# DeltaNet's raw keys, queries and values turned by a DMA exchange through DRAM and VectorE block transposes in place of TensorE transposes

## The chip, the core and the metric

The kernel runs on one core of a Trainium2 chip. A core has a matrix engine (TensorE, PE in the profile), a vector engine (VectorE, DVE), an activation engine (ScalarE, ACT), a general engine (GpSimd, POOL), a queue engine that here only issues transfers (SyncE, SP) and 16 DMA engines between DRAM and the on-chip memory SBUF. TensorE writes to a second on-chip memory, PSUM, that VectorE and ScalarE read. The engines run their own instruction streams and meet at semaphores. The metric is the device time of one execution in microseconds (us).

## The reference, cut to what matters here

One decoder layer over 256 tokens of width 2048: a gated DeltaNet branch with 16 heads of 128 and a sliding-window attention branch, merged by gates, then an output projection and a squared-ReLU MLP. The part that the change touches is the way of queries, keys and values from their projection to the depthwise convolution over time:

```python
def causal_depthwise_conv(x, w):           # w has CONV_K = 4 taps per channel
    return lax.conv_general_dilated(
        x, w[:, None, :].astype(x.dtype), window_strides=(1,), padding=[(w.shape[0] - 1, 0)],
        dimension_numbers=("NWC", "WIO", "NWC"), feature_group_count=x.shape[-1])

h = rms_norm(x, norm1_g[l])
proj = h @ w_in[l]
qkv_g, z, b_logit, a_logit, q_s, k_s, v_s, gate_logits = jnp.split(proj, split_points, axis=-1)
# gdn_branch:
qkv_c = jax.nn.silu(causal_depthwise_conv(qkv, conv_w))
q, k, v = jnp.split(qkv_c, 3, axis=-1)
q = l2_normalize(heads(q))
k = l2_normalize(heads(k))
o = gated_delta_rule(q, k, heads(v), g, beta)
```

The projection leaves tokens on partitions and channels along the row; the convolution works along the tokens with one weight per channel, so its input is wanted with channels on partitions.

## The kernel before

All weights arrive as 584 chunks of 128x1024 floats (512 KB) in a ring of four buffers `raw`. ScalarE rounds a chunk to `w_hi` (L776), VectorE subtracts to get the rest `w_lo` (L1176, the function `split`), and TensorE multiplies three times, in `product`: hi by hi (L347), hi activations by `w_lo` (L348), lo activations by `w_hi` (L349). Both other engines are `AHEAD = 3` chunks ahead of the chunk whose jobs they do. An output of 512 columns takes 8 chunks; its sums stand in one of two halves of PSUM's `acc`.

The first 16 outputs are four windows `w` = 0 to 3 of four outputs each: keys, queries, values and the gate z of one group of four heads. At the end of an output ScalarE (first 128 tokens, L1036) and VectorE (the other 128, L1584) copy it scaled to `rawg[:, n]`. The work on the heads of group g runs between the matmuls of window g + 1, at places given by tables: TensorE counts a step `s` for every three matmuls of `product` (128 in a window; a chunk is four), the other two count `h`, half as fast (64 in a window). `k_step` is also called with `s - 128` and `h - 64`, so a key step at -8 stands 8 steps before the end of the window that makes the keys.

For each item (keys K, queries Q, values V) of a group the way is this. `turn_group` on TensorE transposes `rawg[:, n]` in eight 128x128 pieces into two PSUM banks `J` (L404), at `PE_FRONT`: K at -8, Q at 17, V at 54. `conv` on ScalarE makes the first tap from `J` (L832, four instructions), `tap` on VectorE adds three more taps (L1207, four instructions each), for K at h = -5, 0 and 4. ScalarE takes a tanh (L849), `silu` on VectorE multiplies (L1213), and `turn_units` on TensorE turns the result back (L411), at `PE_BACK`: K at 17, directly ahead of the turn of Q; then come norms and the delta rule's inverse. That inverse goes in five levels: TensorE multiplies (L435, at `PE_INV_V`), VectorE adds (L1220), TensorE squares (L445), VectorE writes under masks (L1226 to L1230), and the next level's L435 waits for that. The L435 of level 2 (they count from 0) is at s = 55, one step behind the turn of V. Later steps are products with the state (`PE_P1` L526, `PE_P2` L540, `PE_P3` L550), which VectorE prepares (L1348) and takes up (L1361, L1366), a final scale that waits for a GpSimd power (L1378), and the turn of the outputs with its rounded parts (L1388 on VectorE).

SyncE issues chunk c as soon as VectorE has split chunk c - 4 (L321 in `stream`).

Of the kernel before, what the change touches and what calls it, by code (L numbers as in the profile page):

```python
# [20 lines left out]
ALU = mybir.AluOpType  # L21
# [13 lines left out]
HG = 4  # L35
# [33 lines left out]

PE_FRONT = {ITEM_K: -8, ITEM_Q: 17, ITEM_V: 54}  # L70
PE_BACK = {ITEM_K: 17, ITEM_Q: 49, ITEM_V: 80}
# [37 lines left out]
def hybrid_trunk(nc, x, weights, w_ba, colp_d, rowp_d, masks_d, dist_d, fgain_d, out):  # L109
    with ExitStack() as ctx:  # L110
# [56 lines left out]
        with ExitStack() as mlp:  # L167
# [92 lines left out]
        def over(a, n, b=None):  # L260
# [16 lines left out]
        rawg_a, rawg_d, cw_ready, par_ready = sem("rawg_a"), sem("rawg_d"), sem("cw_ready"), sem("par_ready")  # L277
        front_T, conv_0, conv_tap, tanh_done, silu_done, back_T = (
            sem(n) for n in ("front_T", "conv_0", "conv_tap", "tanh_done", "silu_done", "back_T"))
        vb_done, nsq_done, nssq_done, nr_link, nr_done, norm_done = (  # L280
# [27 lines left out]
        @block.sync  # L308
        def _(sp):
            for i in range(4):  # L310
                sp.dma_start(raw[:, i], weights[i]).then_inc(raw_in[i], 16)
                for n in ((0, 1) if i == 0 else (i + 1,)):
                    cols = X_COLS[n]
                    sp.dma_start(xres[:, :, cols], x[:, :, cols]).then_inc(x_in[n], 16)

            def stream(a, b):
# [8 lines left out]
            stream(1, first_swa)  # L325
# [15 lines left out]
        def _(pe):  # L341
# [57 lines left out]

            def turn_group(src, b0, sem_, dst_cols=None):  # L400

                for m in range(HG):
                    for t in range(NT):
                        ins = tr(J[:, b0 + m // 2, (m % 2) * T + t * P:(m % 2) * T + (t + 1) * P],  # L404
                                 src[:, t, m * P:(m + 1) * P], ident)
                ins.then_inc(sem_, 1)

            def turn_units(b0, src, done):
# [5 lines left out]
            def k_step(s, g):  # L414

                if s == PE_FRONT[ITEM_K]:
                    pe.wait_ge(rawg_a, 4 * g + 1)
                    pe.wait_ge(rawg_d, 4 * g + 1)

                    pe.wait_ge(o_done, NCH * g + NCH)  # L420
                    turn_group(rawg[:, ITEM_K], BANK[ITEM_K], front_T)
                if s == PE_BACK[ITEM_K]:
                    pe.wait_ge(silu_done, 4 * g + 1)
                    turn_units(0, kU, back_T)
# [33 lines left out]
            def gdn_step(s, g):  # L458
# [6 lines left out]
                if s == PE_KK:  # L465
# [4 lines left out]
                    inner(0, False, kk_done)  # L470
                if s == PE_FRONT[ITEM_Q]:
                    pe.wait_ge(rawg_a, 4 * g + 2)
                    pe.wait_ge(rawg_d, 4 * g + 2)

                    pe.wait_ge(exp_done, g + 1)
                    turn_group(rawg[:, ITEM_Q], 2, front_T)
# [7 lines left out]
                if s == PE_FRONT[ITEM_V]:  # L484
                    pe.wait_ge(rawg_a, 4 * g + 3)
                    pe.wait_ge(rawg_d, 4 * g + 3)

                    pe.wait_ge(nsq_done, 2 * g + 2)
                    turn_group(rawg[:, ITEM_V], 2, front_T)
                if s == PE_BACK[ITEM_V]:  # L490
# [273 lines left out]
        def _(act):  # L764
# [63 lines left out]
            def conv(n, g, dst):  # L828

                act.wait_ge(front_T, 3 * g + (n + 1))  # L830
                for m in range(HG):
                    ins = A(dst[:, m], J[:, BANK[n] + m // 2, (m % 2) * T:(m % 2 + 1) * T], ACT.Copy,  # L832
                            scale=cwg[:, n, m, 3:4])
                ins.then_inc(conv_0, 1)
# [186 lines left out]
            def window(q0, jobs):  # L1021
                for n in range(4):
                    def ops(n=n):
# [11 lines left out]
                        else:  # L1035
                            A(rawg[:, n, 0], acc[:, n % 2, 0], ACT.Copy, scale=row_scale(0, 0)).then_inc(rawg_a, 1)  # L1036
                    output(q0 + n * (CPO // RING), jobs, read(q0 + (n + 1) * (CPO // RING), ops), h0=16 * n,
# [24 lines left out]
            for n in range(5):  # L1062
                def ops(n=n):
                    if n == 0:

                        act.wait_ge(front_T, 3 * NG - 2)
                        A(kdup[:, 0].rearrange("p (k d c) -> p k d c", k=4, d=2),
# [98 lines left out]
        def _(dve):  # L1166
# [32 lines left out]
            def tap(n, s, g, dst):  # L1199
# [5 lines left out]
                for m in range(HG):  # L1205
                    b, o = BANK[n] + m // 2, (m % 2) * T
                    ins = stt(out=dst[:, m, s:T], in0=J[:, b, o:o + T - s], scalar=cwg[:, n, m, 3 - s:4 - s],  # L1207
                              in1=dst[:, m, s:T], op0=ALU.mult, op1=ALU.add)
# [13 lines left out]
            def write_xu(lv, g):  # L1222
# [669 lines left out]
```

## Time and profile before

| | |
|---|---|
| median of 3 runs | 1782.39 us (1782.3 to 1782.4) |
| the profiled execution | 1781.72 us, its span 1779.8 us |
| TensorE busy | 1762.3 us (99%), granted clock 0.999 |
| VectorE busy | 1264.3 us (71%) |
| ScalarE busy | 853.1 us (48%) |
| GpSimd busy | 96.3 us (5%) |
| bytes moved by DMA | 316.49 MB, mean 178 GB/s |

Busy time is the union of an engine's instructions. Matmuls overlap, since the next one enters before the last has drained; a 512-column matmul is shown with about 0.39 us but the next begins about 0.23 us after it, so a short stop of TensorE can hide under the tail of the matmul before. The four windows of DeltaNet's projections end at about 109, 226, 344 and 461 us of the span; the work on group 3 runs on to about 575 us beside the next outputs.

### The profile page before, as it was taken

Reading aid. Unit: us, or ns where it says so; the run is one execution under the profiler, and the core shown is the slowest. Engines: PE = TensorE matmul, PEld = TensorE weight load, DVE = VectorE, ACT = ScalarE, POOL = GpSimd, SP = SyncE. Lnnn points to the kernel's source line nnn. Section 1 sums busy time; section 2 is a strip of 40 time slices with the busy share of each in tenths; the row PEclk is TensorE's granted clock in tenths of the full one; section 3 lists DMA queues with packets and bytes.
Section 4 is the critical chain, followed back from the end, with each engine's and each line's share of the span. In section 5 each row is a group of like instructions: output and inputs, shape, how many; then the busy total and the mean of one; then the engine's idle time right before and its main releaser. Section 6 shows DMA issues by size and latency. Waiting matters only on the chain.

```text
span 1779.8 us, 27113 instructions
## 1 busy us (share of the span) xinstructions
PE 1762.3 (99%) x9974; PEld 1432.9 (81%) x9974; DVE 1264.3 (71%) x1903; ACT 853.1 (48%) x1345; POOL 96.3 (5%) x81
## 2 busy tenths in 40 slices
PE   8999999999999999999999999999999999999998
PEld 6887787777777888888888888888888888888886
DVE  5578688787886677775676697888644468886444
ACT  6454454554645455554444454454443345444443
POOL 0021030030210000000000000000000000000000
PEclk9999999999999999999999999999999999999999
DMA  7544444444444545445666565555666555556554
GB/s 265 176 156 133 155 151 138 160 143 143 137 136 161 178 153 168 155 154 187 204 210 201 198 217 186 192 189 195 205 191 197 192 192 194 192 189 198 192 191 140
DMA packets 88118, 316.49 MB, mean 178 GB/s; under 512 B 9728, under 2 KB 10496, under 8 KB 87888
## 3 DMA queue, kind: packets, MB, share of 16 engines
q1 hardware_dynamic: 86608, 311.20, 52.6%
q0 software_dynamic: 832, 3.15, 0.5%
q8 instruction: 73, 1.20, 0.3%
q10 hardware_dynamic: 576, 0.71, 0.1%
q14 instruction: 29, 0.24, 0.0%
HBM read 312.92 MB, written 2.10 MB: 177 GB/s over the span
## 4 chain that ended last, share of the span: by engine, by line
PE 93%; DVE 6%; issue 1%; ACT 0%; DMA 0%; POOLq 0%; POOL 0%; ACTq 0%; DVEq 0%
PE acc L347 29%; PE acc L348 28%; PE acc L349 28%; DVE cT L1207 2%; DVE w_lo L1176 1%; PE J L526 1%; PE J L578 1%; PE J L411 1%; PE J L404 1%; PE J L435 1%; PE J L540 1%; PE J L455 0%; PE J L550 0%; PE J L597 0%; PE J L445 0%
## 5 line engine op out<-in xcount | busy, mean ns | idle before, releaser
L1176 DVE TENSOR_TENSOR w_lo<-raw,w_hi 128x1024 fp32r<-128x1024 f32 x584 | 712.5, 1227 | 352.5 <-ACT w_hi L776 349.7
L776 ACT ACTIVATE w_hi<-raw 128x1024 fp32r<-128x1024 f32 x584 | 617.0, 1062 | 648.2 <-PE acc L349 641.3
L347 PE MATMUL acc<-w_hi,hT_hi 128*128 128x512 f32 x1440 | 577.3, 401 | 2.3 <-DVE w_lo L1176 1.5
L348 PE MATMUL acc<-w_lo,hT_hi 128*128 128x512 f32 x1440 | 562.7, 391 | 0.0
L349 PE MATMUL acc<-w_hi,hT_lo 128*128 128x512 f32 x1440 | 561.9, 390 | 0.0
L347 PEld LDWEIGHTS acc<-w_hi,hT_hi 128*128 128x128 f32 x1440 | 270.7, 188 | 67.4 <-issue 7.0
L349 PEld LDWEIGHTS acc<-w_hi,hT_lo 128*128 128x128 f32 x1440 | 270.9, 188 | 57.8
L348 PEld LDWEIGHTS acc<-w_lo,hT_hi 128*128 128x128 f32 x1440 | 271.1, 188 | 52.7 <-issue 1.0
L347 PE MATMUL acc<-w_hi,act_hi 128*128 128x512 f32 x512 | 199.2, 389 | 0.0
L348 PE MATMUL acc<-w_lo,act_hi 128*128 128x512 f32 x512 | 199.2, 389 | 0.0
L349 PE MATMUL acc<-w_hi,act_lo 128*128 128x512 f32 x512 | 199.2, 389 | 0.0
L1483 DVE STREAM_TRANSPOSE nat<-rbuf 32x256 f32<-32x256 f32 x256 | 111.5, 435 | 4.1
L348 PEld LDWEIGHTS acc<-w_lo,act_hi 128*128 128x128 f32 x512 | 96.1, 188 | 20.0
L349 PEld LDWEIGHTS acc<-w_hi,act_lo 128*128 128x128 f32 x512 | 96.1, 188 | 20.0
L347 PEld LDWEIGHTS acc<-w_hi,act_hi 128*128 128x128 f32 x512 | 96.1, 188 | 19.9
L347 PE MATMUL acc<-w_hi,og_hi 128*128 128x512 f32 x256 | 100.5, 392 | 0.0
L349 PE MATMUL acc<-w_hi,og_lo 128*128 128x512 f32 x256 | 99.7, 389 | 0.0
L348 PE MATMUL acc<-w_lo,og_hi 128*128 128x512 f32 x256 | 99.7, 389 | 0.0
L347 PEld LDWEIGHTS acc<-w_hi,og_hi 128*128 128x128 f32 x256 | 48.1, 188 | 11.1 <-issue 1.3
L349 PEld LDWEIGHTS acc<-w_hi,og_lo 128*128 128x128 f32 x256 | 48.1, 188 | 10.1
L348 PEld LDWEIGHTS acc<-w_lo,og_hi 128*128 128x128 f32 x256 | 48.1, 188 | 9.7
L347 PE MATMUL acc<-w_hi,os_hi 128*128 128x512 f32 x128 | 49.8, 389 | 0.0
(234 smaller groups left out, 1341.1 us busy)
## 6 DMA issues: line engine op xcount, KB each, us to landing
raw<-weights SPq DMA_DIRECT2D x584, 512.0 KB, 3.4
xres<-x POOLq DMA_DIRECT2D x4, 512.0 KB, 4.8
xres<-x SPq DMA_DIRECT2D x3, 512.0 KB, 8.9
y<-nat SPq DMA_DIRECT2D x6, 256.0 KB, 3.7
fgain_sb<-fgain SPq DMA_DIRECT2D x1, 1024.0 KB, 5.5
masks_sb<-masks POOLq DMA_DIRECT2D x1, 704.0 KB, 8.1
xres<-x SPq DMA_DIRECT2D x2, 256.0 KB, 5.3
y<-nat ACTq DMA_DIRECT2D x2, 256.0 KB, 3.1
```

The source lines that it names most:

```text
L347: mm(o, aT_hi[:, kt, tok], w_hi[:, c % RING, w], start=first, stop=False)
L348: mm(o, aT_hi[:, kt, tok], w_lo[:, c % RING, w], start=False, stop=False)
L349: return mm(o, aT_lo[:, kt, tok], w_hi[:, c % RING, w], start=False, stop=last)
L404: ins = tr(J[:, b0 + m // 2, (m % 2) * T + t * P:(m % 2) * T + (t + 1) * P], src[:, t, m * P:(m + 1) * P], ident)
L411: ins = tr(J[:, b0 + u // HG, (u % HG) * P:(u % HG + 1) * P], src[:, u * P:(u + 1) * P], ident)
L435: ins = mm(J[to, bank, a * C:(a + 1) * C], lhs[r, 2 * a + b], rhs[r, 2 * a + b], start=True, stop=True)
L526: ins = mm(J[rows(par ^ q), 0, (2 * q + m) * P:(2 * q + m + 1) * P], head(src, c, 2 * m + par), S[:, 2 * m + par], start=True, stop=True)
L540: ins = mm(J[rows(par ^ q), bank, m * P:(m + 1) * P], solve[r, 2 * c + m, q], RH[r, m * P:(m + 1) * P] if c else vb3[r, m], start=True, st ...
L776: A(w_hi[:, slot], raw[:, slot], ACT.Copy).then_inc(hi_ready, 1)
L1176: tt(w_lo[:, slot], raw[:, slot], w_hi[:, slot].bitcast(F32), ALU.subtract).then_inc(lo_ready, 1)
L1207: ins = stt(out=dst[:, m, s:T], in0=J[:, b, o:o + T - s], scalar=cwg[:, n, m, 3 - s:4 - s], in1=dst[:, m, s:T], op0=ALU.mult, op1=ALU.add)
L1483: return V.transpose(dst[to * Q:(to + 1) * Q].rearrange("p (a t q n) -> p q t a n", a=4, t=NT, q=P // Q)[:, at], src[at * Q:(at + 1) * Q]. ...
```

## The change

TensorE's `turn_group` goes, with the table `PE_FRONT`. The copies of an output to `rawg` (K, Q, V) now write each quarter of 32 channels of the four heads side by side. SyncE writes `rawg[:, n]` to a DRAM buffer (`front_write`, one DMA of 512 KB) at chunk 17, 25 or 33 counted from the window's first, and two chunks later reads it back (`front_read`, eight DMAs of 32 partitions x 4 runs x 512 bytes) with partition quarters and channel quarters exchanged, into the last four rows of `og_hi` or `og_lo`, which no group but the last uses. VectorE then transposes all blocks of 32x32 with one instruction of 128x1024 (`take_front`), back into `rawg[:, n]`, at h = 37 (K), 46 (Q) and 61 (V) of the window that makes them. `conv` and `tap` read that in SBUF and not `J`.

```diff
-PE_FRONT = {ITEM_K: -8, ITEM_Q: 17, ITEM_V: 54}
+DVE_FRONT = {ITEM_K: 37, ITEM_Q: 46, ITEM_V: 61}
+SP_OUT, SP_BACK = (17, 25, 33), (19, 27, 35)
+        fronts = [a[:, 12:16].rearrange("p a t -> p (a t)").bitcast(F32) for a in (og_hi, og_lo)]
+        bounce = [nc.dram_tensor(f"bounce{i}", (P, NT * NB), F32, kind="Internal").ap() for i in range(2)]
...
+            def front_write(k):
+                w, n = divmod(k, 3)
+                sp.wait_ge(rawg_a, 4 * w + n + 1)
+                sp.wait_ge(rawg_d, 4 * w + n + 1)
+                if k > 1:
+                    sp.wait_ge(front_T, k - 1)
+                sp.dma_start(bounce[k % 2], rawg[:, n].rearrange("p t n -> p (t n)")).then_inc(front_out, 16)
+            def front_read(k):
+                sp.wait_ge(front_out, 16 * (k + 1))
+                if k:
+                    sp.wait_ge(front_T, k)
+                kept = bounce[k % 2].rearrange("(q j) (t p f) -> j p t q f", j=Q, t=NT, p=P // Q)
+                for p in range(P // Q):
+                    for t in range(NT):
+                        sp.dma_start(fronts[k % 3 % 2][p * Q:(p + 1) * Q].rearrange("j (t q f) -> j t q f", t=NT, q=P // Q)[:, t],
+                                     kept[:, p, t]).then_inc(front_in, 16)
...
-                if s == PE_FRONT[ITEM_K]:
-                    pe.wait_ge(rawg_a, 4 * g + 1)
-                    pe.wait_ge(rawg_d, 4 * g + 1)
-
-                    pe.wait_ge(o_done, NCH * g + NCH)
-                    turn_group(rawg[:, ITEM_K], BANK[ITEM_K], front_T)
...
-                    ins = A(dst[:, m], J[:, BANK[n] + m // 2, (m % 2) * T:(m % 2 + 1) * T], ACT.Copy,
-                            scale=cwg[:, n, m, 3:4])
+                    ins = A(dst[:, m], front(n)[:, m], ACT.Copy, scale=cwg[:, n, m, 3:4])
...
-                            A(rawg[:, n, 0], acc[:, n % 2, 0], ACT.Copy, scale=row_scale(0, 0)).then_inc(rawg_a, 1)
+                            A(by_quarter(rawg[:, n, 0]), by_head(acc[:, n % 2, 0]), ACT.Copy,
+                              scale=row_scale(0, 0)).then_inc(rawg_a, 1)
...
-                    ins = stt(out=dst[:, m, s:T], in0=J[:, b, o:o + T - s], scalar=cwg[:, n, m, 3 - s:4 - s],
+                    ins = stt(out=dst[:, m, s:T], in0=front(n)[:, m, 0:T - s], scalar=cwg[:, n, m, 3 - s:4 - s],
...
+            def take_front(n, g):
+                k = 3 * g + n
+                dve.wait_ge(front_in, 16 * 8 * (k + 1))
+                V.transpose(front(n).rearrange("p m (b j) -> p b m j", j=Q),
+                            fronts[n % 2].rearrange("p (b m i) -> p b m i", m=HG, i=Q)).then_inc(front_T, 1)
+
             def k_step(h, g):
+                for n in (ITEM_K, ITEM_Q, ITEM_V):
+                    if h == DVE_FRONT[n] - STEPS:
+                        take_front(n, g)
```

Where the three new instructions fall is seen at three places. The first is VectorE at the end of window 1, from the final scale of group 0 (L1378) to the rounded outputs (L1388); L1176 is `split`, L1207 the first tap on K of group 1. Before:

```order
L1378 SCALAR_TENSOR_TENSOR qn<-qn,rg,zs 128x128 [waits silu_done,or_done]
L1378 SCALAR_TENSOR_TENSOR qn<-qn,rg,zs 128x128 x7
L1176 TENSOR_TENSOR w_lo<-raw,w_hi 128x1024 [waits hi_ready]
L1207 SCALAR_TENSOR_TENSOR cT<-J,cwg,cT 128x255 [waits conv_0]
L1207 SCALAR_TENSOR_TENSOR cT<-J,cwg,cT 128x255 x3
L1176 TENSOR_TENSOR w_lo<-raw,w_hi 128x1024 [waits hi_ready] x2
L1388 SCALAR_TENSOR_TENSOR og_lo<-J,colp_sb,og_hi 128x256 [waits og_hi_done,o_T]
```

And the same place in the changed kernel, whose lines are numbered anew (L1412 is the scale, L1201 `split`, L1231 the tap, L1264 `take_front`):

```order
L1412 SCALAR_TENSOR_TENSOR qn<-qn,rg,zs 128x128 x7
L1201 TENSOR_TENSOR w_lo<-raw,w_hi 128x1024 [waits hi_ready]
L1231 SCALAR_TENSOR_TENSOR cT<-rawg,cwg,cT 128x255 [waits conv_0]
L1231 SCALAR_TENSOR_TENSOR cT<-rawg,cwg,cT 128x255 x3
L1201 TENSOR_TENSOR w_lo<-raw,w_hi 128x1024 [waits hi_ready]
L1264 STREAM_TRANSPOSE rawg<-og_hi 128x8x4x32 [waits front_in]
L1201 TENSOR_TENSOR w_lo<-raw,w_hi 128x1024 [waits hi_ready]
L1422 SCALAR_TENSOR_TENSOR og_lo<-J,colp_sb,og_hi 128x256 [waits og_hi_done,o_T]
```

The transpose of V stands between the two splits, in the middle of the taps on K; nothing else has moved. The second place is TensorE around the turn of V (L404) and level 2 of the inverse (L435) in window 1. Before:

```order
L347 MATMUL acc<-w_hi,hT_hi 128x512
L348 MATMUL acc<-w_lo,hT_hi 128x512
L349 MATMUL acc<-w_hi,hT_lo 128x512
L404 MATMUL J<-masks_sb,rawg 128x128 [waits nsq_done,rawg_d,rawg_a]
L404 MATMUL J<-masks_sb,rawg 128x128 x7
L347 MATMUL acc<-w_hi,hT_hi 128x512
L348 MATMUL acc<-w_lo,hT_hi 128x512
L349 MATMUL acc<-w_hi,hT_lo 128x512
L435 MATMUL J<-mats 64x64 [waits inv_done,bt_ready]
```

After (L472 is what L435 was, L398 to L400 are `product`):

```order
L398 MATMUL acc<-w_hi,hT_hi 128x512
L399 MATMUL acc<-w_lo,hT_hi 128x512
L400 MATMUL acc<-w_hi,hT_lo 128x512
L472 MATMUL J<-mats 64x64 [waits inv_done,bt_ready]
L472 MATMUL J<-mats 64x64 x15
```

The eight transposes are gone from ahead of L435, whose waits are the same. The third place is the queue of SyncE, for the values of one window; before, it held only the chunks (L321). After:

```order
L363 DMA raw<-weights 128x1024 [waits lo_ready] x6
L340 DMA bounce<-rawg 128x1024 [waits front_T,rawg_d,rawg_a]
L363 DMA raw<-weights 128x1024 [waits lo_ready] x2
L350 DMA og_hi<-bounce 32x4x128 [waits front_T,front_out]
L350 DMA og_hi<-bounce 32x4x128 x7
```

The write stands two chunks ahead of the eight reads, and both stand between the chunks in one queue.

## Rows read from the trace of the kernel before

**Rows 1.** The page: the span, and the chain that ended last by engine
```profile
span 1779.8 us, 27113 instructions
...
PE 93%; DVE 6%; issue 1%; ACT 0%; DMA 0%; POOLq 0%; POOL 0%; ACTq 0%; DVEq 0%
```

**Rows 2.** Windows: stretch, length, busy us (instructions) of each engine, clock, DMA share, GB/s
```profile
105.00:222.00 117.00, 116.56 (x993) 90.78 (x992) 93.10 (x168) 59.68 (x129) 19.62 (x15) 1.00 0.42 141
```

**Rows 3.** Chain in order of time: start us, us, what; the turn of V
```profile
155.84 0.87 PE J L404 x8
```

**Rows 4.** Timeline of TensorE, window 1: start us, us, engine, line, op, shape, count
```profile
155.68 1.04 PE L404 MATMUL J<-masks_sb,rawg 128*128 128x128 f32 x8
...
157.34 0.69 PE L435 MATMUL J<-mats 64*64 64x64 f32 x32
```

**Rows 5.** Timeline of VectorE: the write that L435 of level 2 waits for
```profile
156.12 0.91 DVE L1230 COPY_PREDICATED zs<-masks_sb,J 64x256 f32<-64x256 uint32 x2
```

**Rows 6.** Timeline of VectorE, end of window 1, idle before and releaser in brackets
```profile
217.20 2.19 DVE L1378 SCALAR_TENSOR_TENSOR qn<-qn,rg,zs 128x128 f32<-128x128 f32 x8 [1.75 <-POOL rg L1752]
219.31 1.22 DVE L1176 TENSOR_TENSOR w_lo<-raw,w_hi 128x1024 fp32r<-128x1024 f32 x1
221.38 1.65 DVE L1207 SCALAR_TENSOR_TENSOR cT<-J,cwg,cT 128x255 f32<-128x255 f32 x4 [0.85 <-ACT cT L832]
222.95 2.35 DVE L1176 TENSOR_TENSOR w_lo<-raw,w_hi 128x1024 fp32r<-128x1024 f32 x2
...
237.14 1.43 DVE L1213 SCALAR_TENSOR_TENSOR kq<-vb,cT 128x256 f32<-128x256 f32 x4
```

**Rows 7.** Timeline of TensorE: the matmul before the turn back of K, and that turn
```profile
238.12 0.39 PE L349 MATMUL acc<-w_hi,hT_lo 128*128 128x512 f32 x1
238.62 1.09 PE L411 MATMUL J<-masks_sb,kq 128*128 128x128 f32 x8
```

**Rows 8.** The line L411: idle of its engine before it, us, times
```profile
  DVE kq L1213: 1.6, 3
```

**Rows 9.** Timeline of ScalarE: the first tap on K of group 1
```profile
219.78 1.57 ACT L832 ACTIVATE cT<-J,cwg 128x256 f32<-128x256 f32 x4 [3.22 <-PE J L404]
```

**Rows 10.** Groups by form, VectorE: busy us, mean ns, then idle before
```profile
L1176 DVE TENSOR_TENSOR w_lo<-raw,w_hi 128x1024 fp32r<-128x1024 f32 x584 | 712.5, 1227 | 352.5 <-ACT w_hi L776 349.7
L1483 DVE STREAM_TRANSPOSE nat<-rbuf 32x256 f32<-32x256 f32 x256 | 111.5, 435 | 4.1
...
L1378 DVE SCALAR_TENSOR_TENSOR qn<-qn,rg,zs 128x128 f32<-128x128 f32 x32 | 8.8, 347 | 7.0 <-POOL rg L1752 7.0
...
L1355 DVE SCALAR_TENSOR_TENSOR qn<-J,scg,mats 128x128 f32<-128x128 f32 x24 | 7.3, 347 | 17.6 <-ACT mats L905 17.6
```

**Rows 11.** The line L321, 105 to 480 us: issue ns min/median/max, time to landing
```profile
L321 SPq DMA_DIRECT2D raw<-weights x102: 332/333/576, 108.1 to 474.8; - x102
...
DMA to landing us min/median/max: 3.0/3.4/5.3
```

**Rows 12.** Timeline of SyncE: the issue behind which the reads of V now stand
```profile
212.20 0.33 SPq L321 DMA_DIRECT2D raw<-weights  x1
```

**Rows 13.** Timeline of VectorE, end of window 0: first tap and silu of K, group 0
```profile
105.14 1.65 DVE L1207 SCALAR_TENSOR_TENSOR cT<-J,cwg,cT 128x255 f32<-128x255 f32 x4 [3.56 <-ACT cT L832]
...
119.51 1.43 DVE L1213 SCALAR_TENSOR_TENSOR kq<-vb,cT 128x256 f32<-128x256 f32 x4
```

**Rows 14.** Timeline of TensorE: the turn back of K, group 0
```profile
121.20 1.04 PE L411 MATMUL J<-masks_sb,kq 128*128 128x128 f32 x8
```

**Rows 15.** Timeline of VectorE, group 3: its shortest wait for level 0 of the inverse
```profile
499.25 0.69 DVE L1220 TENSOR_TENSOR mats<-zs,J 128x512 f32<-128x512 f32 x1 [1.31 <-PE J L435]
```

**Rows 16.** Timeline of VectorE, window 1: where the transposes of K and Q fall
```profile
187.43 0.42 DVE L1361 COPY S<-J 128x256 f32<-128x256 f32 x1 [2.98 <-PE J L550]
...
202.30 0.60 DVE L1348 SCALAR_TENSOR_TENSOR mats<-J,scg,vb 128x128 f32<-128x128 f32 x2
```

**Rows 17.** Timeline of TensorE: the product that waits for that L1348
```profile
204.71 0.67 PE L540 MATMUL J<-mats,solve 64*64 64x128 f32 x16
```

More of the change, by code:

```diff
@@ L224, in hybrid_trunk, with by_quarter, by_head, front @@
         kdup = rawg[:, 0]
+        def by_quarter(a):
+            return a.rearrange("p (q m i) -> p m q i", q=P // Q, m=HG)
+        def by_head(a):
+            return a.rearrange("p (m q i) -> p m q i", q=P // Q, m=HG)
+        def front(n):
+            return rawg[:, n].rearrange("p t n -> p (t n)").rearrange("p (h t) -> p h t", h=HG)
         def mat(i):
@@ L277, in hybrid_trunk @@
         rawg_a, rawg_d, cw_ready, par_ready = sem("rawg_a"), sem("rawg_d"), sem("cw_ready"), sem("par_ready")
-        front_T, conv_0, conv_tap, tanh_done, silu_done, back_T = (
-            sem(n) for n in ("front_T", "conv_0", "conv_tap", "tanh_done", "silu_done", "back_T"))
+        front_out, front_in, front_T = sem("front_out"), sem("front_in"), sem("front_T")
+        conv_0, conv_tap, tanh_done, silu_done, back_T = (
+            sem(n) for n in ("conv_0", "conv_tap", "tanh_done", "silu_done", "back_T"))
         vb_done, nsq_done, nssq_done, nr_link, nr_done, norm_done = (
@@ L314, in _, with groups @@
                     sp.dma_start(xres[:, :, cols], x[:, :, cols]).then_inc(x_in[n], 16)
+            def front_write(k):
[14 more added lines that the diff above has]
+                                     kept[:, p, t]).then_inc(front_in, 16)
+            def groups(a, b):
+                for c in range(a, b):
+                    for n in range(3):
+                        for w in range(NG):
+                            if c == 4 * CPO * w + SP_OUT[n]:
+                                front_write(3 * w + n)
+                            if c == 4 * CPO * w + SP_BACK[n]:
+                                front_read(3 * w + n)
+                    sp.wait_ge(lo_ready, c - RING + 1)
+                    sp.dma_start(raw[:, c % RING], weights[c]).then_inc(raw_in[c % RING], 16)
             def stream(a, b):
@@ L324, in _ @@
             first_swa = OUT_MIX1 * CPO // RING
-            stream(1, first_swa)
+            last_front = 4 * CPO * (NG - 1) + SP_BACK[ITEM_V] + 1
+            groups(RING, last_front)
+            stream(last_front // RING, first_swa)
             sp.wait_ge(og_lo_done, 2 * NG + 2)
@@ L398, in turned_by @@
                 return lambda c: pe.wait_ge(turn_lo, 8 * k + c + 1)
[L400 to L406, printed above, removed]
             def turn_units(b0, src, done):
@@ L470, in gdn_step @@
                     inner(0, False, kk_done)
[L471 to L476, printed above, removed]
                 if s == PE_KQ:
@@ L483, in gdn_step @@
                     turn_units(2, qU, back_T)
[L484 to L489, printed above, removed]
                 if s == PE_BACK[ITEM_V]:
@@ L1064, in ops @@
                     if n == 0:
-                        act.wait_ge(front_T, 3 * NG - 2)
+                        act.wait_ge(conv_tap, 9 * (NG - 1) + 3)
                         A(kdup[:, 0].rearrange("p (k d c) -> p k d c", k=4, d=2),
@@ L1583, in ops @@
                         else:
-                            ts(rawg[:, n, 1], acc[:, n % 2, 1], row_scale(0, 1), None, ALU.mult).then_inc(rawg_d, 1)
+                            ts(by_quarter(rawg[:, n, 1]), by_head(acc[:, n % 2, 1]), row_scale(0, 1), None,
+                               ALU.mult).then_inc(rawg_d, 1)
                     output(q0 + n * (CPO // RING), jobs, read(q0 + (n + 1) * (CPO // RING), ops), h0=16 * n,
@@ L1604, in ops @@
                     if n == 0:
-                        dve.wait_ge(front_T, 3 * NG - 2)
+                        dve.wait_ge(conv_0, 3 * (NG - 1) + 1)
                         ts(kdup[:, 1].rearrange("p (k d c) -> p k d c", k=4, d=2),
```

1 line of the change is left out of this document (removed).

## The prediction

> **What bounds the kernel now.** I read the chain first: 93% of it is TensorE, 6% VectorE [rows 1]. Then the windows, to see whether that share is even: in window 1 TensorE is busy 116.56 of 117.00 us and VectorE 93.10 us, at full clock, with the DMA engines at 0.42 [rows 2]. So removed TensorE work is worth its full length only where VectorE, which there has but 24 us to spare, does not then arrive last. Third, the two timelines around each removed turn, for the wait that comes next on TensorE. The reader is to see there two places where VectorE delivers at the very moment, or later than, TensorE asks: before the turn back of K and before level 2 of the inverse.
>
> **What is removed.** A turn of eight transposes takes 0.87 us of the chain [rows 3]; twelve of them are 10.4 us, the most that the change can give back directly. The rest of this part asks at each of the three sites how much of it stays.
>
> *Turn of V (four times).* Three matmuls behind it stands L435 of level 2, which now starts at 157.34 [rows 4]. Without the turn TensorE would be there at 157.34 - 0.87 = 156.47. But it waits for VectorE's masked write, which ends at 156.12 + 0.91 = 157.03 [rows 5]; from VectorE's end to TensorE's start takes 0.05 us where one is seen waiting for the other (237.14 + 1.43 = 238.57, then 238.62) [rows 6, 7]. So it starts at 157.08 and 0.26 us stays of 0.87. Four times: -1.04 us.
>
> *Turn of Q (four times).* It follows the turn back of K directly. Behind it VectorE works without a pause until it waits for TensorE at level 0 of the inverse, and the shortest of these four waits is 1.31 us [rows 15]. TensorE comes there 0.87 us sooner and that wait shrinks to 0.44 us, so the whole piece stays: 4 x 0.87 = -3.48 us.
>
> *Turn of K, group 0.* Silu ends at 119.51 + 1.43 = 120.94 and TensorE starts its turn back at 121.20 [rows 13, 14]. VectorE idled 3.56 us before its first tap, waiting for ScalarE and through it for the turn [rows 13]. The tap's input is now ready long before, and 3.56 us take in the new transpose (below) with ease, so VectorE is early enough: -0.87 us.
>
> *Turn of K, groups 1 to 3.* Here it comes out the other way. TensorE's matmul before the turn back starts at 238.12, the turn back at 238.62 [rows 7], and the profile names silu as what ended the idle time before L411 in three cases [rows 8]: VectorE is last already. Its work from 219.31 to 238.57 has one gap, 0.85 us before the first tap [rows 6], which ScalarE caused, itself idle 3.22 us for the turn on TensorE [rows 9]. This gap goes: -0.85. Into the same stretch comes the transpose of V: + its length. TensorE gains nothing by arriving earlier; it starts when silu ends.
>
> **What is added on VectorE.** Twelve block transposes of 128x1024. No row shows one. A 128x1024 subtraction takes 1.23 us; a transpose of 32x256 takes 0.435 us, that is at most 4 x 0.435 = 1.74 us for rows four times as long [rows 10]. I take 1.25 us, near the low end, because 0.435 us is mostly 256 elements at the subtraction's pace plus a start. The range keeps 1.23 to 1.74. The Vector Engine (DVE) Microarchitecture Reference of the Trainium skill (section 3.8) says that the 32x32 transpose sustains one element per cycle per lane; no run here shows it for 128 partitions, and by it the value would also be near 1.25.
>
> The transpose of V costs 3 x (1.25 - 0.85) = +1.20 us in groups 1 to 3. The stretch before it starts from a fixed point, the scale that waited 1.75 us for GpSimd [rows 6], so nothing upstream pays for it. The transpose of K lies before a wait of 2.98 us for TensorE [rows 16]: nothing; without that wait it would be 1.25 us each. The transpose of Q delays L1348, which ends at 202.30 + 0.60 = 202.90 [rows 16], to 204.15, and TensorE's product that wants it starts at 204.71 [rows 17]: nothing, with 0.5 us to spare, and at 1.74 us just nothing.
>
> **What else changes.** Taps read SBUF where they read PSUM: an operation of the same form costs 347 ns with either [rows 10], so nothing. The copies to `rawg` in runs of 32 elements have the same count of elements; I take nothing, and a small cost would fall outside the two tight stretches. SyncE issues nine DMAs more for an item. An issue takes 0.333 us, 0.576 at most [rows 11], so eight reads hold the queue 2.7 to 4.6 us. The weight chunk behind them is that much later; it lands 3.4 us after its issue [rows 11], while ScalarE reads it a ring of four chunks later, 4 x 117.00 / 32 = 14.6 us [rows 2], so this hides too; the cover gone, each us of it would be one of the whole.
>
> *Does the exchange arrive?* The tightest is V. Its reads stand behind the chunk issued at 212.20 [rows 12], so they begin at 212.53, are all issued at 215.2 to 217.1 and, with landing times of 3.0 to 5.3 us [rows 11], have landed at 218.2 to 222.4. VectorE wants them after the split that follows the first tap: 219.31 + 1.22 + 1.65 + 1.17 (half of 2.35) = 223.3 [rows 6]. On time, by 0.9 us at worst.
>
> **Sum.** -0.87 (K, group 0) + 1.20 (K, groups 1 to 3, with the transpose of V) - 3.48 (Q) - 1.04 (V) = -4.19 us. Against the profiled execution, 1781.72 - 4.19 = 1777.5; its 1781.72 lies 0.67 us under the median of the runs shown, so against the median 1782.39 - 4.19 = **1778.2 us**, 0.24% less. Of 10.4 us removed 40% are kept.
>
> **Rivals.** *All is kept.* If VectorE catches up in ways that two timelines don't show, each turn gives its 0.87 us: 1782.39 - 10.4 = 1772.0. For it: TensorE is 93% of the chain. Against it: the idle before L411 [rows 8]. Half way lies a transpose that hides in groups 1 to 3 and leaves only the gap's gain: 3 x (-0.85) in place of +1.20, sum -7.9, 1774.5.
>
> *The transpose is dear.* At 1.74 us groups 1 to 3 cost 3 x 0.89 = 2.67 in place of 1.20: sum -2.7, 1779.7, inside 0.2%. At 2.5 us (two passes) they cost 4.95 and Q's transpose another 3 x 0.75 = 2.25: sum +1.8, 1784.2. Only the former is within my rows.
>
> *The exchange of V comes late, and the kernel is slower.* A DMA of short runs may land later than the rows of weights do. The point is 223.3, and every microsecond beyond it delays silu on K in three groups: 3 us per us. The gain is gone when the last read lands at 223.3 + 4.19 / 3 = 224.7, that is 12.2 us after the first issue where my worst sum gives 9.9; at 226.5 it is +5.4 us against the median, 1787.8. For it: eight transfers of 512-byte runs behind one queue, beside weights. Against it: half of the DMA engines' time is free [rows 2]. On this side speaks the Trainium skill too: VectorE: DVE Perf Modes (Rules for kernel authors) sends a 128x128 transpose whose target may be PSUM to TensorE, and DMA: Bandwidth & Descriptors (Anatomy of one DMA) warns that the write receipt, most for DRAM, can be a surprisingly long delay; the write has two chunks to land in, and the trace holds no write to DRAM beside the weights to test that.
>
> *Removed work turns into waiting everywhere,* Q included: then only group 0's pieces stay, about -2 us, 1780.4, no measurable change.
>
> **Chances.** A measurement of this kernel tells 0.2%, 3.6 us, from no change; the bounds are 1778.8 and 1786.0. The forecast as worked out, 1777 to 1779.5: 0.48. More is kept, 1772 to 1777: 0.19. Less is kept or the transpose is dear, 1779.5 to 1785: 0.21. Late exchange or a transpose of two passes, slower than 1786: 0.12. The forecast's case straddles the bound, two thirds of it below, so faster is 0.32 + 0.19 = 0.51; slower 0.12; the same 0.37. The range, 1773.5 to 1784.0, leaves out the end of the first rival and the late exchange.
>
> **What would show each step.** TensorE's matmul instructions fewer by 96 and no turn between the matmuls. STREAM_TRANSPOSE of 128x1024 at 1.25 us, twelve times. The turn back of K in groups 1 to 3 waiting longer than before for silu, and VectorE without a gap from the scale to silu; group 0's without that wait. L435 of level 2 waiting for the masked write some 0.6 us. The waits of VectorE for level 0 near 0.4 to 1 us. No wait of VectorE for the DMA at the transposes. I am wrong if the transpose of V waits for its reads, if its length is over 1.74 us, or if L411 starts no later relative to the scale L1378 than now.

## The result and the profile after

The changed kernel takes **1788.9 us** (median of 6 runs, 1788.7 to 1790.1), the kernel before 1782.3 us beside it (median of 6): a ratio of 1.004, 95% interval 1.003 to 1.005. It is 6.6 us slower where the forecast was 4.2 us faster, and lies above the range. The profiled execution took 1789.2 us, its span 1787.3 us.

The page of the profile after, span and busy time; its chain by engine answers to [rows 1]:

```profile
span 1787.3 us, 26636 instructions
...
PE 1754.8 (98%) x9878; PEld 1422.1 (80%) x9878; DVE 1291.4 (72%) x1915; ACT 854.7 (48%) x1345; POOL 100.4 (6%) x81
...
PE 77%; issue 11%; DVE 9%; ACT 2%; POOL 1%; DMA 0%; POOLq 0%; DVEq 0%; SPq 0%
```

TensorE does 7.5 us less work (1762.3 before) and still ends later, so it waits more. VectorE does 27 us more, and that is the first thing to notice: twelve transposes of 1.24 us are only 15. The groups by form show most of the rest. The 11% "issue" of the chain are three pieces of 56 us that the view gives to no wait; the faster variants below have them too (10%), so I read nothing from them. The change shows in VectorE's share of the chain, 9% for 6% [rows 1].

The groups of VectorE by form, the taps (columns as in [rows 10]):

```profile
L1231 DVE SCALAR_TENSOR_TENSOR qn<-rawg,cwg,qn 128x255 f32<-128x255 f32 x16 | 17.1, 1127 | 0.0
L1231 DVE SCALAR_TENSOR_TENSOR cT<-rawg,cwg,cT 128x254 f32<-128x254 f32 x32 | 16.4, 573 | 0.0
...
L1231 DVE SCALAR_TENSOR_TENSOR cT<-rawg,cwg,cT 128x255 f32<-128x255 f32 x32 | 13.3, 478 | 0.4 <-ACT cT L857 0.4
...
L1231 DVE SCALAR_TENSOR_TENSOR qn<-rawg,cwg,qn 128x254 f32<-128x254 f32 x16 | 6.7, 479 | 0.1
```

The taps of one line, on one kind of operand, have nearly the same size, but the first on Q (`qn`, 255 columns) takes 1127 ns on average and its neighbour of 254 columns 479. The second on K and V (`cT`, 254) is raised to 573. A mean hides what happens; the four first taps on Q of one group, taken one by one from the line's own view (duration min/median/max, start), and the timeline of GpSimd over the same time are:

```profile
L1231 DVE SCALAR_TENSOR_TENSOR qn<-rawg,cwg,qn x1: 1260/1260/1260, 126.6 to 126.6; 128x255 f32<-128x255 f32 x1
L1231 DVE SCALAR_TENSOR_TENSOR qn<-rawg,cwg,qn x1: 1509/1509/1509, 127.8 to 127.8; 128x255 f32<-128x255 f32 x1
L1231 DVE SCALAR_TENSOR_TENSOR qn<-rawg,cwg,qn x1: 1261/1261/1261, 129.3 to 129.3; 128x255 f32<-128x255 f32 x1
L1231 DVE SCALAR_TENSOR_TENSOR qn<-rawg,cwg,qn x1: 471/471/471, 130.4 to 130.4; 128x255 f32<-128x255 f32 x1
```

```profile
125.66 1.96 POOL L1799 TENSOR_TENSOR mats<-scg,masks_sb 128x512 f32<-128x512 f32 x1 [0.18 <-DVE scg L1305]
127.58 1.47 POOL L1801 TENSOR_TENSOR mats<-mats,masks_sb 128x512 f32<-128x512 f32 x1
129.01 1.22 POOL L1802 TENSOR_TENSOR mats<-mats,scg 128x512 f32<-128x512 f32 x1
130.20 1.85 POOL L1787 TENSOR_TENSOR rg<-rg,stat 128x8 f32<-128x8 f32 x1
```

Put side by side they interleave. GpSimd's three large instructions end at 127.62, 129.05 and 130.23; the three slow taps end at 127.9, 129.3 and 130.5, each 0.3 us behind one of them. The fourth begins when GpSimd's large work is over and takes 471 ns. So each tap stands until GpSimd's instruction has ended, then runs; GpSimd's next one, begun by then, is itself lengthened by the tap. The three lose 1260 + 1509 + 1261 - 3 x 475 = 2605 ns, in four groups 10.4 us.

The waits of TensorE (us in total, times, longest), the views of VectorE's transposes and SyncE's reads, and TensorE's turn back of K in groups 0 and 1, which answers to [rows 14] and [rows 7]:

```profile
PE acc L398 <- DVE w_lo L1201: 7.4, 12, 1.4
PE J L454 <- DVE kq L1237: 6.5, 4, 2.0
```

```profile
L1264 DVE STREAM_TRANSPOSE rawg<-og_hi x8: 1236/1238/1240, 71.9 to 462.7; 128x1024 f32<-128x1024 f32 x8
```

```profile
L350 SPq DMA_DIRECT2D og_hi<-bounce x64: 377/432/1485, 50.9 to 455.3; - x64
...
DMA to landing us min/median/max: 2.0/2.8/4.0
```

```profile
120.74 1.09 PE L454 MATMUL J<-masks_sb,kq 128*128 128x128 f32 x8 [0.46 <-DVE kq L1237]
...
240.24 1.09 PE L454 MATMUL J<-masks_sb,kq 128*128 128x128 f32 x8 [2.02 <-DVE kq L1237]
```

In group 1 the turn back starts 119.50 us after that of group 0, where before these were 238.62 - 121.20 = 117.42 us apart [rows 7, 14]. No row shows VectorE waiting for a transfer at a transpose.

### The profile page after: what moved, and what is told of

It reads as the page before. It is cut to its first block, busy times and chain, and to the rows that moved or that the text cites. A ratio compares the mean times of both kernels' runs of the same rounds, so it can differ in the third digit from the quotient of the medians.

```text
span 1787.3 us, 26636 instructions
## 1 busy us (share of the span) xinstructions
PE 1754.8 (98%) x9878; PEld 1422.1 (80%) x9878; DVE 1291.4 (72%) x1915; ACT 854.7 (48%) x1345; POOL 100.4 (6%) x81
## 4 chain that ended last, share of the span: by engine, by line
PE 77%; issue 11%; DVE 9%; ACT 2%; POOL 1%; DMA 0%; POOLq 0%; DVEq 0%; SPq 0%
PE acc L398 25%; PE acc L399 24%; PE acc L400 24%; DVE w_lo L1201 3%; DVE qn L1231 2%; DVE cT L1231 1%; PE J L603 1%; ACT w_hi L801 1%; ACT kn L863 0%; ACT qn L863 0%; PE J L622 0%; PE J L614 0%; PE J L472 0%; DVE qn L1412 0%; PE J L613 0%
## 5 line engine op out<-in xcount | busy, mean ns | idle before, releaser
L1201 DVE TENSOR_TENSOR w_lo<-raw,w_hi 128x1024 fp32r<-128x1024 f32 x584 | 714.0, 1228 | 346.8 <-ACT w_hi L801 344.0
L398 PE MATMUL acc<-w_hi,hT_hi 128*128 128x512 f32 x1440 | 577.7, 401 | 8.1 <-DVE w_lo L1201 7.4
L400 PE MATMUL acc<-w_hi,hT_lo 128*128 128x512 f32 x1440 | 562.0, 390 | 0.0
L398 PEld LDWEIGHTS acc<-w_hi,hT_hi 128*128 128x128 f32 x1440 | 270.7, 188 | 76.9 <-DVE w_lo L1201 11.3
L400 PEld LDWEIGHTS acc<-w_hi,hT_lo 128*128 128x128 f32 x1440 | 270.8, 188 | 58.0
L398 PE MATMUL acc<-w_hi,act_hi 128*128 128x512 f32 x512 | 199.2, 389 | 0.0
L400 PE MATMUL acc<-w_hi,act_lo 128*128 128x512 f32 x512 | 199.2, 389 | 0.0
L398 PEld LDWEIGHTS acc<-w_hi,act_hi 128*128 128x128 f32 x512 | 96.1, 188 | 20.0
L400 PEld LDWEIGHTS acc<-w_hi,act_lo 128*128 128x128 f32 x512 | 96.1, 188 | 19.8
L398 PE MATMUL acc<-w_hi,og_hi 128*128 128x512 f32 x256 | 100.5, 393 | 0.0
L400 PE MATMUL acc<-w_hi,og_lo 128*128 128x512 f32 x256 | 99.7, 389 | 0.0
L398 PEld LDWEIGHTS acc<-w_hi,og_hi 128*128 128x128 f32 x256 | 48.1, 188 | 11.1 <-issue 1.3
L400 PEld LDWEIGHTS acc<-w_hi,og_lo 128*128 128x128 f32 x256 | 48.1, 188 | 10.1
L398 PE MATMUL acc<-w_hi,os_hi 128*128 128x512 f32 x128 | 49.8, 389 | 0.0
```

Of the source, the lines that this page charges most:

```text
L398: mm(o, aT_hi[:, kt, tok], w_hi[:, c % RING, w], start=first, stop=False)
L400: return mm(o, aT_lo[:, kt, tok], w_hi[:, c % RING, w], start=False, stop=last)
L1201: tt(w_lo[:, slot], raw[:, slot], w_hi[:, slot].bitcast(F32), ALU.subtract).then_inc(lo_ready, 1)
```

## The experiments

**Taps read PSUM again.** My theory from the rows above was that VectorE's tap, whose two tensor operands both lie in SBUF now, can't go on while GpSimd works on SBUF. This variant gives the taps on the changed kernel their old operand back; the convolution's values are left wrong by it, the instructions, sizes and waits stay.

```diff
-ins = stt(out=dst[:, m, s:T], in0=front(n)[:, m, 0:T - s], ...)
+b, o = BANK[n] + m // 2, (m % 2) * T
+ins = stt(out=dst[:, m, s:T], in0=J[:, b, o:o + T - s], ...)
```

> The changed kernel, its taps on VectorE reading PSUM's J again in place of the turned rows in SBUF (J holds nothing useful there, so the convolution is not computed rightly; every other instruction, the exchange and the twelve block transposes are kept). Theory A, port: a tap with both tensor operands in SBUF is held up while GpSimd works on SBUF. Then the first tap on Q, 1127 ns on average in the changed kernel, returns to about 476 ns, the second tap on K from 573 to 475, and the time falls from 1788.9 to 1777 to 1780, what the sum without this term gave (1778.2). Theory B, exchange: the DMA traffic and SyncE's longer queue delay weights or VectorE; then it stays at 1788 to 1789.

Measured: 1777.7 us (10 runs) against 1781.5, ratio 0.9979 (0.9969 to 0.9989). The tap group, the waits of TensorE, and the turn back of K in groups 0 and 1:

```profile
L1232 DVE SCALAR_TENSOR_TENSOR qn<-J,cwg,qn 128x255 f32<-128x255 f32 x16 | 6.6, 476 | 0.0
```

```profile
PE J L454 <- DVE kq L1238: 3.6, 3, 1.2
PE J L472 <- DVE zs L1255: 2.6, 4, 0.7
PE acc L398 <- DVE w_lo L1201: 1.5, 4, 0.4
```

```profile
119.82 1.03 PE L454 MATMUL J<-masks_sb,kq 128*128 128x128 f32 x8
...
236.36 1.09 PE L454 MATMUL J<-masks_sb,kq 128*128 128x128 f32 x8 [1.19 <-DVE kq L1238]
```

One operand decides the sign. With it in PSUM the change gives 3.8 us, where my sum had 4.2; with it in SBUF the same kernel is 10.4 us worse by the two ratios (11.2 by the medians). GpSimd works beside the taps here as well, and they take 476 ns.

**The kernel before, with its taps on SBUF.** The reverse: nothing of the change but this operand (its values are not the turned ones) and, with it, two waits that guard the reuse of `rawg`.

```diff
-ins = stt(out=dst[:, m, s:T], in0=J[:, b, o:o + T - s], ...)
+ins = stt(out=dst[:, m, s:T], in0=src[:, m, 0:T - s], ...)
```

> The kernel before, with the turns on TensorE and no exchange, only the three later taps on VectorE read rawg in SBUF in place of J (unturned rows, so the convolution is not computed rightly). Theory A, port: the first tap on Q goes from 476 to about 1127 ns, 10.4 us more of VectorE in all, and the time rises from 1782.3 to 1786 to 1790. Theory B, exchange: taps 476 ns and 1782.3.

Measured: 1789.5 us, ratio 1.0046 (1.0029 to 1.0063), 8 us worse than before, and the same lengths as in the changed kernel:

```profile
L1207 DVE SCALAR_TENSOR_TENSOR qn<-rawg,cwg,qn 128x255 f32<-128x255 f32 x16 | 17.1, 1128 | 0.0
L1207 DVE SCALAR_TENSOR_TENSOR cT<-rawg,cwg,cT 128x254 f32<-128x254 f32 x32 | 16.4, 574 | 0.0
```

So neither the exchange nor the transposes are needed for the loss. That it is 8 us here and 10 to 11 there comes from VectorE's idle before level 0 of the inverse, which takes up a part of the delay. In the kernel before these waits are 1.85, 1.70, 1.69 and 1.31 us in groups 0 to 3 (the last is [rows 15]), and here 0.48 in each:

```profile
148.01 0.69 DVE L1220 TENSOR_TENSOR mats<-zs,J 128x512 f32<-128x512 f32 x1 [0.48 <-PE J L435]
```

So 4.6 us of the taps' delay are taken up here. In the changed kernel, against the variant with taps on PSUM (0.94, 0.81, 0.85 and 0.48 us there), it is only 1.1 us. The difference of 3.5 us is what lies between the two losses.

**No exchange.** The changed kernel without the DMAs through DRAM; the transposes turn zeros.

```diff
-sp.dma_start(bounce[k % 2], rawg[:, n]...).then_inc(front_out, 16)
-sp.wait_ge(front_out, 16 * (k + 1))
-for p in range(P // Q):
-    for t in range(NT):
-        sp.dma_start(fronts[k % 3 % 2]..., kept[:, p, t]).then_inc(front_in, 16)
-dve.wait_ge(front_in, 16 * 8 * (k + 1))
+dve.wait_ge(rawg_a, 4 * g + n + 1)
...
+V.memset(fronts[0], 0.0)
+V.memset(fronts[1], 0.0)
```

> The changed kernel without its DMA exchange: no write to DRAM, no read back; the block transposes run on zeros (so keys, queries and values are not computed rightly), taps read SBUF as in the changed kernel. Theory A, port: 1787.5 to 1789, the taps on Q as slow as with the exchange (about 1127 ns). Theory B, exchange: 1777 to 1783.

Measured: 1789.3 us, ratio 1.0043 (1.0026 to 1.006), equal to the changed kernel within the intervals, with the taps as slow as there:

```profile
L1224 DVE SCALAR_TENSOR_TENSOR qn<-rawg,cwg,qn 128x255 f32<-128x255 f32 x16 | 17.1, 1127 | 0.0
```

The intervals leave some 3 us open, but the traces agree far closer: from the turn back of K in group 0 to that in group 3 there are 358.33 us here (119.95 to 478.28) and 358.48 in the changed kernel (120.74 to 479.22). The exchange costs nothing that can be measured, and transfers are not what slows the taps.

**GpSimd later.** What is left as a rival is that the first tap on Q is slow by itself. Here GpSimd holds its beta rows back until two of the three taps on Q are through.

```diff
 pool.wait_ge(beta_done, g + 1)
+pool.wait_ge(conv_tap, 9 * g + 5)
 tt(mat(M_B0), wide(scu(BETA), C), over(eye64, U), ALU.mult).then_inc(rows_rhs, 1)
```

> The changed kernel, with one wait added: GpSimd starts its beta rows of a head group only once VectorE has issued the first two taps on Q. Theory (VectorE's tap with both tensor operands in SBUF can't go on while GpSimd works on SBUF): the first tap on Q falls from a mean of 1127 ns to near 476, since GpSimd is idle beside it; the second tap on K (573 ns) may stay or not. Rival (the first tap on Q is slow for a reason of its own, such as its operand's buffer or the DMA that reads the same tile): it stays at 1127 ns. The time is no test: GpSimd's rows come later by some 8 us a group, and TensorE's work on the gates may wait for them; between 1783 and 1795 us.

Measured: 1793.4 us, ratio 1.0065 (1.005 to 1.008). The taps on Q by form:

```profile
L1231 DVE SCALAR_TENSOR_TENSOR qn<-rawg,cwg,qn 128x253 f32<-128x253 f32 x16 | 17.0, 1119 | 0.0
...
L1231 DVE SCALAR_TENSOR_TENSOR qn<-rawg,cwg,qn 128x255 f32<-128x255 f32 x16 | 6.6, 475 | 0.0
```

GpSimd's rows moved, and the slowness moved with them: now the third tap (253 columns) takes 1119 ns and the first 475. So the cause is GpSimd's work beside the tap, not the tap itself. The fix itself is no good, since TensorE now waits for GpSimd's rows:

```profile
PE J L506 <- POOL mats L1800: 7.4, 4, 2.2
```

**No transpose of V.** The changed kernel with taps on PSUM, and V's block transpose reduced to clearing one column, to price the term of groups 1 to 3.

```diff
 def take_front(n, g):
+    if n == ITEM_V:
+        V.memset(rawg[:, n, 0, 0:1], 0.0).then_inc(front_T, 1)
+        return
```

> The changed kernel with the taps reading PSUM (1777.7 us) and V's block transpose replaced by a memset of one column; it leaves the turning of V out. Theory (the block transposes on V, behind the taps, stand on VectorE's path to TensorE's turn back of K in the three windows beside recurrence work): three fewer of 1.25 us there take up to 3.75 us, 1774.0 us, and the idle of TensorE at the turn back behind the K silu falls from 3.6 us to near 0. Rival (VectorE catches up before TensorE asks): within 1 us of 1777.7.

Measured: 1774.4 us, ratio 0.9961 (0.9946 to 0.9976), 3.3 us under the variant with it; the wait for the K silu is gone from TensorE's list:

```profile
PE J L472 <- DVE zs L1255: 2.6, 4, 0.7
PE acc L398 <- DVE w_lo L1201: 1.5, 4, 0.4
```

So the transpose on the path is 3.3 / 3 = 1.1 us a window of its 1.24.

**A version that computes the same and is faster.** The transposes write their result to the banks of `J` in PSUM, so the taps read PSUM, and each is done just before its taps, at places where VectorE waited anyway (K ahead of the final scale, Q and V at h = 6 and 27 of the next window). The reads of K and V are issued later, ScalarE's first tap on V moves from h = 26 to 28, and the waits that guard the buffers follow; the cut shows the main lines.

```diff
-DVE_FRONT = {ITEM_K: 37, ITEM_Q: 46, ITEM_V: 61}
-SP_OUT, SP_BACK = (17, 25, 33), (19, 27, 35)
+DVE_FRONT_K, DVE_FRONT = 56, {ITEM_Q: 6, ITEM_V: 27}
+SP_OUT, SP_BACK = (17, 25, 33), (23, 27, 39)
...
-return rawg[:, n].rearrange("p t n -> p (t n)").rearrange("p (h t) -> p h t", h=HG)
+b = BANK[n]
+return J[:, b:b + 2].rearrange("p b n -> p (b n)").rearrange("p (h t) -> p h t", h=HG)
```

> Exchange kept, but VectorE's block transposes write PSUM's J and stand in its idle time: K ahead of the final scale where it waits 1.75 us for GpSimd, Q ahead of the wait of 2.3 us for ScalarE's norms of K, V ahead of the wait of 2.4 us for level 2; conv and taps read J as in the kernel before; the read back moves to chunks 23, 27 and 39. Theory A, port: taps at 476 ns everywhere; K 0.87 + 3 x 0.85, Q 4 x 0.87, V 4 x 0.26, together 7.9 us less than before: 1773.5 to 1776. Theory B, exchange: the exchange still costs its 10 us, 1784 or more.

Measured: 1774.0 us, ratio 0.9957 (0.994 to 0.9973); again, beside the next experiment, 1773.8 us, ratio 0.9955 (0.9942 to 0.9969). A transpose to PSUM takes as long as one to SBUF, and ahead of the final scale it lies in the wait for GpSimd, of which 0.58 us are left where there were 1.75 [rows 6]:

```profile
L1265 DVE STREAM_TRANSPOSE J<-og_hi 128x1024 f32<-128x1024 f32 x8 | 10.0, 1255 | 0.0
```

```profile
213.58 1.25 DVE L1265 STREAM_TRANSPOSE J<-og_hi 128x1024 f32<-128x1024 f32 x1
...
215.41 2.19 DVE L1417 SCALAR_TENSOR_TENSOR qn<-qn,rg,zs 128x128 f32<-128x128 f32 x8 [0.58 <-POOL rg L1792]
```

**One step of TensorE's table.** On top of that, level 2 of the inverse one step later, where TensorE waits 0.65 us a group since the turn of V is gone.

```diff
-PE_INV_V = (46, 50, 55, 67, 72)
+PE_INV_V = (46, 50, 56, 67, 72)
```

> The kernel with the transposes written to PSUM in idle places of VectorE (1774.0 us), with TensorE's third step of the inverse work placed one step later. Theory (the wait of 0.65 us in each of four groups at the squares behind VectorE's row is idle of TensorE for good): it goes, 4 x 0.65 = 2.6 us, 1771.4 us. Rival (the next level's wait grows by as much): 1774 us, with the wait at another line.

Its neighbour for comparison, the kernel of the experiment before:

> The same kernel as e5_transpose_to_psum, beside the others on the same chip: 1774.0 us, within 0.5 us.

Measured: 1771.3 us (5 runs), ratio 0.9942 (0.9929 to 0.9956), against 1773.8 for the neighbour (1773.6 to 1774.5). All runs of the one lie below all of the other. The wait for `zs` is not in the list any more:

```profile
PE J L444 <- DMA xres<-x: 7.7, 2, 6.6
PE acc L399 <- DVE w_lo L1202: 1.5, 4, 0.4
```

## Why the prediction was wrong

The step that failed is one sentence: "Taps read SBUF where they read PSUM: an operation of the same form costs 347 ns with either [rows 10], so nothing." Both rows are true, and neither says what was asked. VectorE's L1378 and L1355 were taken as if an operation had one length; the row with both operands in SBUF was one during which GpSimd did nothing, for it had just finished the power that L1378 waits for. The first taps on Q stand beside three GpSimd instructions, the second on K beside one. What it cost there:

- From one turn back of K to the next the changed kernel takes 119.50 us where the variant with taps on PSUM takes 236.36 - 119.82 = 116.54. From group 0 to group 3 these are 479.22 - 120.74 = 358.48 and 469.59 - 119.82 = 349.77: 8.7 us.
- K, groups 1 to 3, is 0.84 us of each of these three: 1.65 us of taps become 2.45, and the turn back starts 240.24 - 217.81 = 22.43 us behind the final scale where with taps on PSUM it was 236.36 - 214.77 = 21.59.
- Q is the rest, 2.1 us each. The taps lose 2.61 us, and VectorE's wait before level 0 of the inverse gives back a part (in group 0 it is 0.94 us in the variant with taps on PSUM, 0.48 in the changed kernel).
- Q, group 3: behind its turn back the changed kernel's span has 1787.3 - 479.22 = 1308.1 us left, the variant's 1775.3 - 469.59 = 1305.7: 2.4 us. The wait before level 0 is 0.48 us in that variant already and has nothing to give.
- K, group 0: TensorE now waits 0.46 us at the turn back, where it did not wait with taps on PSUM.
- Together 8.7 + 2.4 + 0.46 = 11.5 us. The runs give 10.4 by ratios and 11.2 by medians.

The rows these numbers are read from, one of TensorE and then those of VectorE, first the changed kernel, then the variant with taps on PSUM:

```profile
479.22 1.09 PE L454 MATMUL J<-masks_sb,kq 128*128 128x128 f32 x8 [2.03 <-DVE kq L1237]
...
147.41 0.69 DVE L1244 TENSOR_TENSOR mats<-zs,J 128x512 f32<-128x512 f32 x1 [0.48 <-PE J L472]
...
217.81 2.19 DVE L1412 SCALAR_TENSOR_TENSOR qn<-qn,rg,zs 128x128 f32<-128x128 f32 x8 [1.75 <-POOL rg L1787]
...
231.04 2.45 DVE L1231 SCALAR_TENSOR_TENSOR cT<-rawg,cwg,cT 128x254 f32<-128x254 f32 x4
```

```profile
469.59 1.09 PE L454 MATMUL J<-masks_sb,kq 128*128 128x128 f32 x8 [1.18 <-DVE kq L1238]
...
144.54 0.69 DVE L1245 TENSOR_TENSOR mats<-zs,J 128x512 f32<-128x512 f32 x1 [0.94 <-PE J L472]
...
214.77 2.19 DVE L1413 SCALAR_TENSOR_TENSOR qn<-qn,rg,zs 128x128 f32<-128x128 f32 x8 [1.75 <-POOL rg L1788]
216.87 1.22 DVE L1201 TENSOR_TENSOR w_lo<-raw,w_hi 128x1024 fp32r<-128x1024 f32 x1
218.00 1.65 DVE L1232 SCALAR_TENSOR_TENSOR cT<-J,cwg,cT 128x255 f32<-128x255 f32 x4
...
228.10 1.65 DVE L1232 SCALAR_TENSOR_TENSOR cT<-J,cwg,cT 128x254 f32<-128x254 f32 x4
```

None of my rivals was this one, though the trace of before had it to see. Two groups of GpSimd there have one form, and differ by 0.9 us:

```profile
L1764 POOL TENSOR_TENSOR mats<-scg,masks_sb 128x512 f32<-128x512 f32 x4 | 7.8, 1958 | 2.5 <-DVE scg L1271 2.5
...
L1756 POOL TENSOR_TENSOR mats<-scg,masks_sb 128x512 f32<-128x512 f32 x4 | 4.2, 1046 | 114.7 <-DVE scg L1252 114.7
```

The timelines of before, VectorE's row and then GpSimd's, show what stood beside L1764:

```profile
126.18 1.22 DVE L1176 TENSOR_TENSOR w_lo<-raw,w_hi 128x1024 fp32r<-128x1024 f32 x1
```

```profile
126.34 1.95 POOL L1764 TENSOR_TENSOR mats<-scg,masks_sb 128x512 f32<-128x512 f32 x1 [0.63 <-DVE scg L1271]
```

A split, both of whose operands lie in SBUF, had begun 0.16 us before it and ended at 127.40; GpSimd ended 0.89 us after that, where it needs 1.05 alone. It is the same stop, the other way round, and behind it the first taps on Q already ran beside three instructions of GpSimd: they start at 127.31 and L1764 and the two behind it end at 130.57.

The Trainium skill states the rule too, and I had not weighed it: SBUF — State Buffer (SBUF: two separate sides, Reading the diagram) calls the port pair that VectorE and GpSimd share "an exclusive lock, not a bandwidth split", and counts a VectorE operation with two SBUF inputs beside a GpSimd one that reads SBUF among those that take it; by its section Who interferes with whom an operation with at most one SBUF input and outside the two-port modes does not contend. The interleaving above agrees, in both directions, and so do the 476 ns with one operand in PSUM. By that rule and the timelines of before, three taps on Q and one on K a group would have stopped, which is what the changed kernel shows.

The other steps, by the variant with taps on PSUM:

- *Sum of the rest:* -3.8 measured for -4.19. The interval (0.9969 to 0.9989 is -5.5 to -2.0 us) is too wide to test the single terms, so these are read from the traces.
- *Length of the transpose:* 1.24 us for 1.25. The range of 1.23 to 1.74 and the second rival rested on it; the low end was true.
- *K, groups 1 to 3:* from the final scale to the turn back, 21.42 us before [rows 6, 7], 21.59 now: +0.17 for the +0.40 of the sum. Up to the first tap it is 221.38 - 217.20 = 4.18 before and 218.00 - 214.77 = 3.23 now, so the gap was worth 0.95 and not 0.85; from there to the turn back 17.24 and 18.36, so the transpose costs 1.12 and not 1.25. Records of VectorE that follow each other without a gap overlap by 0.09 us (216.87 + 1.22 = 218.09, and the tap begins at 218.00), and the sum added up recorded lengths. Leaving the transpose out gave the same 1.1 us a window. The mechanism was right, its size somewhat too dear.
- *K, group 0:* TensorE starts its turn back without a wait, at 119.82 for 121.20, as the mechanism has it. How much of the 1.38 us is the forecast's 0.87 can't be told: the turn of K is at 102.41 us in the kernel before and at 101.97 in its variant with taps on SBUF, though nothing ahead of it differs.
- *V:* TensorE waits 0.65 us in each group at level 2, as forecast (0.6), and the last experiment brings back 2.4 of the 2.6 us that these waits make.
- *Q and V together:* from the turn back of K in group 0 to the final scale, 217.20 - 121.20 = 96.00 us before and 214.77 - 119.82 = 94.95 now: -1.05 for -0.87 - 0.26 = -1.13. VectorE's waits at level 0 (0.94, 0.81, 0.85, 0.48 us) lie within the forecast 0.4 to 1. One reading was wrong without harm: behind the turn of Q VectorE does not work without a pause, it waits 2.41 us for ScalarE's norms of K (L1265 in the rows below); that wait hangs on the turn back of K and not on the turn of Q.
- *The exchange:* it arrives. The reads land 2.8 us after their issue (4.0 at most), less than the 3.0 to 5.3 I took from the weights [rows 11]. Reads are issued in 0.43 us, not 0.333. The third rival, the only one that ended slower, did not come about; the kernel is slower, but not by its mechanism.
- *All is kept* (1772.0) is nearly what the best variant reaches, 1771.3 against 1781.6, once the new transposes are in VectorE's idle places and one step of the table is moved: 10.2 us for the 10.4 removed. There TensorE's list of waits holds nothing that it did not hold before, so each removed turn counts in full. It is that rival's number, reached by moving the new work and not by VectorE catching up where the changed kernel has it.

## What to carry to other kernels

A change of the memory that an operand is read from is not free because the instruction's length alone is equal: look up, at every place where it stands, what GpSimd does at the same time. A row's mean says this only if its neighbours were busy in the same way; where several instructions of one form differ twofold, take them one by one and lay the other engines' timelines beside them. And put the work that takes a removed piece's place into a wait that is already there: V's transposes cost 3.3 us in a tight stretch, and with all twelve in VectorE's waits the time (1774.0 us) is that of the variant without V's (1774.4).

## What the runs showed of the hardware

- VectorE's operation on two SBUF operands and a GpSimd instruction of 128x512 exclude each other: the tap takes up to 1509 ns for 475, GpSimd 1.47 us for 1.30 (1.22 for 1.05). In the rows shown, the one that began later was the one that waited. The taps with one operand in PSUM (475 to 478 ns) were not touched. Whether it is GpSimd's reads or its writes that hold VectorE, no run separates.
- Two operands are not needed for it. A TENSOR_SCALAR on `rg`, 128x8 with its one tensor operand in SBUF, took 1.27 us in the kernel before, where it began 0.07 us behind a GpSimd instruction and ended 0.04 us after it. In the changed kernel it began 0.14 us before such an instruction (L1795) ended, took 0.17 us and ended 0.03 us after it. Its lengths are alike in all four groups (1.27 to 1.29 us, and 0.17). The RECIPROCAL on 128x8 behind it took 0.20 us in either kernel, though in the changed one it ran beside GpSimd's L1796 (124.18 to 125.49), so not every VectorE operation is held. The first two rows are of the kernel before, the third of the changed one:

```profile
124.41 1.30 POOL L1761 TENSOR_TENSOR mats<-mats,masks_sb 128x512 f32<-128x512 f32 x1
...
124.48 1.27 DVE L1265 TENSOR_SCALAR rg<-rg 128x8 f32<-128x8 f32 x1 [2.41 <-ACT kn L839]
...
124.09 0.17 DVE L1299 TENSOR_SCALAR rg<-rg 128x8 f32<-128x8 f32 x1 [2.27 <-ACT kn L863]
```

- The transposes to PSUM were not touched: that of Q at 121.20, beside a GpSimd instruction of 128x512 (120.58 to 122.44), took 1.26 us like the others. Those to SBUF stood beside no GpSimd instruction, so no run shows what they do there.
- GpSimd's power on 128x8 (L1787), 1.85 us long in the record, did not hold the fourth tap, 471 ns beside it. So not every GpSimd instruction blocks for its whole recorded length.
- A 128x1024 fp32 block transpose on VectorE takes 1.24 us to SBUF and 1.255 to PSUM, close to the 1.23 of a subtraction of that size; the write of 512 KB to DRAM lands 5.1 us after its issue (6.9 at most), beside the weights.
